# Scratch reads over 128 partitions in column quarters, and a rotation laid out one operation at a time

## What is computed

```
h += 0.5 * swiglu(rms_norm(h), w_in, w_out)      # d_ff 2816
h += mixer(rms_norm(h))                          # layer 0: S5, layer 1: stick-breaking attention
h += 0.5 * swiglu(rms_norm(h), w_in, w_out)
swiglu(h) = (silu(gate) * up) @ w_out            # gate, up = split(h @ w_in)
```

## Time and profile before

| | us |
|---|---|
| median of 3 runs | 1008.85 (1007.89 to 1010.25) |
| the profiled execution | 1011.95 |
| its span | 1010.2 |

### The profile page before, as it was taken

The page is one execution under the profiler, slowest core; times in us unless marked ns, Lnnn a source line. Parts: engine busy times, 40 slices in busy tenths (PEclk is TensorE's granted clock), DMA queues, the critical chain, the costliest instruction groups (busy, mean ns, idle before and its releaser), DMA issues.

```text
span 1010.2 us, 18856 instructions
## 1 busy us (share of the span) xinstructions
PE 986.0 (98%) x7242; PEld 900.6 (89%) x7242; DVE 737.0 (73%) x922; ACT 585.8 (58%) x807; POOL 105.7 (10%) x139
## 2 busy tenths in 40 slices
PE   8998899999999999999999999999999999999997
PEld 8998898988899988888898888888899898888886
DVE  5786786789977777777677777776566687666666
ACT  7543446765355655555456555554599765555555
POOL 4910158100001100000010000001000010000000
PEclk9999999999999999999999999999999999999999
DMA  7879655452246566665646566556643246666563
GB/s 253 216 224 199 185 170 164 145 180 94 63 149 207 163 197 186 192 195 181 198 148 210 188 188 188 188 185 187 191 145 121 88 147 209 189 190 188 194 187 113
DMA packets 50520, 176.89 MB, mean 175 GB/s; under 512 B 7056, under 2 KB 7056, under 8 KB 49936
## 3 DMA queue, kind: packets, MB, share of 16 engines
q1 hardware_dynamic: 50016, 175.32, 57.5%
q10 hardware_dynamic: 432, 0.55, 0.1%
HBM read 174.67 MB, written 1.18 MB: 174 GB/s over the span
## 4 chain that ended last, share of the span: by engine, by line
PE 73%; DVE 10%; DMA 6%; ACT 4%; POOL 4%; issue 3%; SPq 1%; DVEq 0%; POOLq 0%; ACTq 0%
PE mx L1449 11%; PE gu L1449 11%; PE mx L1452 6%; PE gu L1452 5%; DMA raw<-wstream_dram 5%; PE acc L1491 4%; PE gu L1434 4%; PE gu L1435 4%; PE gu L1436 4%; DVE w_lo L909 3%; PE acc L1495 2%; PE gu L1491 2%; ACT w_hi L410 2%; PE mx L1491 2%; PE acc L1478 2%
## 5 line engine op out<-in xcount | busy, mean ns | idle before, releaser
L909 DVE TENSOR_TENSOR w_lo<-raw,w_hi 128x1024 fp32r<-128x1024 f32 x258 | 319.4, 1246 | 107.8 <-ACT w_hi L410 107.1
L410 ACT ACTIVATE w_hi<-raw 128x1024 fp32r<-128x1024 f32 x259 | 271.0, 1052 | 93.5 <-DMA raw<-wstream_dram 34.9
L1434 PE MATMUL gu<-g,w_hi 128*128 128x256 f32 x560 | 161.0, 288 | 4.2 <-DVE w_lo L909 2.4
L1435 PE MATMUL gu<-g,w_hi 128*128 128x256 f32 x560 | 158.4, 283 | 0.0
L1436 PE MATMUL gu<-g,w_lo 128*128 128x256 f32 x560 | 158.3, 283 | 0.0
L1449 PE MATMUL mx<-g,w_hi 128*128 128x512 f32 x480 | 119.9, 392 | 0.0
L1449 PE MATMUL gu<-g,w_hi 128*128 128x512 f32 x464 | 116.1, 392 | 0.0
L1434 PEld LDWEIGHTS gu<-g,w_hi 128*128 128x128 f32 x560 | 107.2, 191 | 5.7 <-issue 3.5
L1435 PEld LDWEIGHTS gu<-g,w_hi 128*128 128x128 f32 x560 | 107.3, 192 | 0.1
L1436 PEld LDWEIGHTS gu<-g,w_lo 128*128 128x128 f32 x560 | 107.2, 192 | 0.0
L1449 PEld LDWEIGHTS mx<-g,w_hi 128*128 128x128 f32 x480 | 87.0, 189 | 16.0
(11 more groups left out here) (325 smaller groups left out, 1912.1 us busy)
## 6 DMA issues: line engine op xcount, KB each, us to landing
raw<-wstream_dram SPq DMA_DIRECT2D x318, 512.0 KB, 3.8
s_memory<-b_turned_dram SPq DMA_DIRECT2D x8, 256.0 KB, 6.6
s_memory<-powers_dram SPq DMA_DIRECT2D x16, 128.0 KB, 8.0
x<-x_in_dram SPq DMA_DIRECT2D x4, 256.0 KB, 6.1
raw<-wstream_dram SPq DMA_DIRECT2D x3, 256.0 KB, 5.8
out_dram<-x_tok SPq DMA_DIRECT2D x3, 256.0 KB, 2.0
gain_row<-last_gain_dram SPq DMA_DIRECT2D x1, 512.0 KB, 4.2
raw<-wstream_dram ACTq DMA_DIRECT2D x1, 256.0 KB, 5.0
```

The lines of the kernel that those rows point to most:

```text
L410: act.activation(weights(unit)[0], raw[:, s_raw, :], ACT.Copy).then_inc(hi_ready, 1)
L909: dve.tensor_tensor(lo, raw[:, n % RAW, :], hi.bitcast(F32), ALU.subtract).then_inc(lo_ready, 1)
L1434: pe.matmul(dst, a, hi, start=start, stop=False, skip_group_check=check)
L1435: pe.matmul(dst, a, lo, start=False, stop=False, skip_group_check=check)
```

## The change

Four things change. The layout of the scratch array: step first, then the half of the pair, so that a store writes two runs (one for each of two steps) where it wrote one. The reads of powers: one copy per unit, over all 128 partitions, of one quarter of the columns (512 floats, 2 KB a row), with the DRAM side as 8 rows each repeated 16 times; the real part comes with units 25 to 28, the imaginary with 29 to 32, each with a counter of its own. The reads of inputs: as many as before, each over 128 partitions and one quarter of the columns, with the DRAM side as 32 rows repeated four times. In the first stage's order, `pad_now` comes one turn earlier (`NOW_TURN` 13), and the six operations of the last doubling stand in turns 18, 19 and 20, one before `scale_gu` and one after it in each, where they stood three and three behind `hidden_low` of turns 18 and 19.

```diff
--- before.py
+++ after.py
@@ -59,7 +59,8 @@
 
 STEP_ARRAYS, S5_ARRAYS = 4, 5
 POWERS_TURNED, POWERS_STORED, POWERS_READ, INPUTS_READ = 5, 24, range(25, 33), range(9, 25, 2)
-OUT_PAD_TURNS, NOW_TURN = (6, 7, 9, 10), 14
+READ_COLS = 512
+OUT_PAD_TURNS, NOW_TURN = (6, 7, 9, 10), 13
 IN_PADS = {17: ((0,), (1,)), 18: ((2,), (3, 4)), 19: ((), (5,)), 20: ((6,), (7,))}
 GROUP, STATE = 16, 64
 PAIRS = 32
@@ -70,7 +71,7 @@
 QP = PAIRS // QUARTERS
 PAIR_ORDER = (0, 4, 1, 5, 2, 6, 3, 7)
 BLOCKS = PAIRS // 4
-FIRST_PRODUCT, KERNEL_TURN, FIRST_ROTATED, DECAY_TURN = 3, 15, 16, 19
+FIRST_PRODUCT, KERNEL_TURN, FIRST_ROTATED, LAST_ROTATED, DECAY_TURN = 3, 15, 16, 18, 19
 SMALL_ROTATIONS = 4
 WARM_UP = 12
 
@@ -229,7 +230,8 @@
         par_ready, par_act, par_dve = sem("par_ready"), sem("par_act"), sem("par_dve")
         powers_ready, dense_ready, padded = sem("powers_ready"), sem("dense_ready"), sem("padded")
         powers_turned, powers_copied = sem("powers_turned"), sem("powers_copied")
-        powers_stored, powers_loaded, inputs_loaded = sem("powers_stored"), sem("powers_loaded"), sem("inputs_loaded")
+        powers_stored, inputs_loaded = sem("powers_stored"), sem("inputs_loaded")
+        powers_loaded = [sem("powers_re_loaded"), sem("powers_im_loaded")]
         c_negated, c_zero_ready, in_dense_ready = sem("c_negated"), sem("c_zero_ready"), sem("in_dense_ready")
         now_cleared, now_dense, in_now_ready = sem("now_cleared"), sem("now_dense"), sem("in_now_ready")
         out_cleared, rot_half = sem("out_cleared"), sem("rot_half")
@@ -315,7 +317,7 @@
 
             return isinstance(i, int) and i == TURNS - 1 and m == BODY - 1
 
-        powers_dram = nc.dram_tensor("powers_dram", (2, STEPS, 2, PAIRS, STATE), F32, kind="Internal").ap()
+        powers_dram = nc.dram_tensor("powers_dram", (STEPS, 2, 2, PAIRS, STATE), F32, kind="Internal").ap()
 
         block = ctx.enter_context(nc.Block())
 
@@ -357,21 +359,22 @@
                 sp.wait_ge(powers_copied, 1)
                 for k in range(2):
                     for g2 in range(2):
-                        sp.dma_start(powers_dram[g2, 2 * k:2 * k + 2].rearrange("j r a p -> (j r a) p"),
+                        sp.dma_start(powers_dram[2 * k:2 * k + 2, g2],
                                      powers_rows[:, P * k + STATE * g2:P * k + STATE * (g2 + 1)]).then_inc(
                             powers_stored, 16)
 
-            def read_powers(r, j):
-                if r == 0 and j == 0:
+            def read_powers(r, part):
+                if r == 0 and part == 0:
                     sp.wait_ge(powers_stored, 16 * 4)
-                for g2 in range(2):
-                    first = CH * j + GROUP * g2
-                    sp.dma_start(powers_t[r][first:first + GROUP, :],
-                                 powers_dram[g2, j, r:r + 1].rearrange("r a p -> r (a p)").broadcast_to(
-                                     [GROUP, PAIRS * STATE])).then_inc(powers_loaded, 16)
-
-            def read_inputs(r, j):
-                sp.dma_start(in_t[r][CH * j:CH * (j + 1), :], b_turned[r]).then_inc(inputs_loaded, 16)
+                cols = slice(READ_COLS * part, READ_COLS * (part + 1))
+                rows = powers_dram[:, :, r].rearrange("j g a p -> (j g) (a p)")[:, cols]
+                sp.dma_start(powers_t[r][:, cols],
+                             rows.unsqueeze(1).broadcast_to([2 * STEPS, GROUP, READ_COLS])).then_inc(powers_loaded[r], 16)
+
+            def read_inputs(r, part):
+                cols = slice(READ_COLS * part, READ_COLS * (part + 1))
+                sp.dma_start(in_t[r][:, cols], b_turned[r:r + 1, :, cols].broadcast_to(
+                    [STEPS, CH, READ_COLS])).then_inc(inputs_loaded, 16)
 
             turns, spread = UNITS // RAW, POWERS_READ[-1] // RAW + 1
             for unit in range(2 * RAW, RAW * spread):
@@ -1095,11 +1098,11 @@
                 real = dense[0].rearrange("p a j h -> p (a j h)")
                 if k == 0:
                     dve.wait_ge(inputs_loaded, 16 * 2 * STEPS)
-                    dve.wait_ge(powers_loaded, 16 * 2 * STEPS)
+                    dve.wait_ge(powers_loaded[0], 16 * STEPS)
                     dve.wait_ge(padded, 4)
                     dve.tensor_tensor(real, powers_t[0], in_t[0], ALU.mult)
                 elif k == 1:
-                    dve.wait_ge(powers_loaded, 16 * 4 * STEPS)
+                    dve.wait_ge(powers_loaded[1], 16 * STEPS)
                     dve.tensor_tensor(spare, powers_t[1], in_t[1], ALU.mult)
                 elif k == 2:
                     step(dve.tensor_tensor(powers_t[0], powers_t[0], in_t[1], ALU.mult))
@@ -1111,19 +1114,28 @@
                     dve.wait_ge(in_dense_ready, 1)
                     dve.tensor_tensor(powers_t[0], real, spare, ALU.subtract).then_inc(in_dense_ready, 1)
 
-            def s5_rotation(k, r):
+            def s5_rotation(k, r, part):
 
                 n = 2 ** k
                 t = [rotation_tmp(k)[:, i, :, 0:n] for i in range(2)]
-                re, im = rot[:, 0, :, 0:n], rot[:, 1, :, 0:n]
+                parts = rot[:, 0, :, 0:n], rot[:, 1, :, 0:n]
                 l_re, l_im = (par[:, i, :].unsqueeze(2).broadcast_to([P, PAIRS, n]) for i in ROTATIONS[k])
-                if r == 0:
-                    dve.tensor_tensor(t[0], re, l_re, ALU.mult)
-                    step(dve.tensor_tensor(t[1], im, l_im, ALU.mult))
+                if part == 0:
+                    dve.tensor_tensor(t[0], parts[r], l_re, ALU.mult)
+                elif part == 1:
+                    step(dve.tensor_tensor(t[1], parts[1 - r], l_im, ALU.mult))
                 else:
-                    dve.tensor_tensor(t[0], im, l_re, ALU.mult)
-                    step(dve.tensor_tensor(t[1], re, l_im, ALU.mult))
-                step(dve.tensor_tensor(rot[:, r, :, n:2 * n], t[0], t[1], (ALU.subtract, ALU.add)[r]))
+                    step(dve.tensor_tensor(rot[:, r, :, n:2 * n], t[0], t[1], (ALU.subtract, ALU.add)[r]))
+
+            def last_rotation(f, part):
+
+                if 0 <= f - LAST_ROTATED < 3:
+                    i = 2 * (f - LAST_ROTATED) + part
+                    if i == 0:
+                        dve.wait_ge(kernels_done, 2)
+                    s5_rotation(SMALL_ROTATIONS + 1, i // 3, i % 3)
+                    if i == 5:
+                        dve.sem_inc(rot_ready, 1)
 
             def read_kernels(half):
                 dve.wait_ge(zeroed, 1)
@@ -1148,22 +1160,21 @@
                     out_product(f - FIRST_PRODUCT)
                 elif 6 <= f - FIRST_PRODUCT < 12:
                     in_product(f - FIRST_PRODUCT - 6)
+                last_rotation(f, 0)
                 scale_gu(f % 2, g0 + 2)
+                last_rotation(f, 1)
                 if KERNEL_TURN < f <= KERNEL_TURN + 2:
                     read_kernels(f - KERNEL_TURN - 1)
                 hidden_high(f % 2, f + 1)
                 split_after(g0 + 1)
                 hidden_low(f % 2, f + 1, f % 2)
-                if 0 <= f - FIRST_ROTATED < 4:
+                if 0 <= f - FIRST_ROTATED < 2:
                     if f == FIRST_ROTATED:
                         dve.wait_ge(rot_started, 1)
-                    if f == FIRST_ROTATED + 2:
-                        dve.wait_ge(kernels_done, 2)
-                    s5_rotation(SMALL_ROTATIONS + (f - FIRST_ROTATED) // 2, (f - FIRST_ROTATED) % 2)
+                    for part in range(3):
+                        s5_rotation(SMALL_ROTATIONS, f - FIRST_ROTATED, part)
                     if f == FIRST_ROTATED + 1:
                         dve.sem_inc(rot_half, 1)
-                    if f == FIRST_ROTATED + 3:
-                        dve.sem_inc(rot_ready, 1)
 
             def add_squares(n):
```

## The result

| | before | after |
|---|---|---|
| median of 13 runs each, us | 1008.77 (1006.2 to 1011.1) | 1011.81 (1010.3 to 1014.2) |
| the profiled execution / its span | 1011.95 / 1010.2 | 1012.66 / 1010.9 |

The ratio is 1.0034 [1.0023, 1.0045]: the change makes the kernel 3.0 us slower by the medians, and 2.3 to 4.5 us by the interval. The forecast was 1003.1, in a range from 996 to 1009, with 0.74 on faster. The profiled execution of before happened to lie 3.2 us above its median and the one after 0.9 above, so the two traces differ by only 0.7 us. They are good for the question where, and the medians for the question how much.

What follows compares the result with a forecast made beforehand. TensorE, busy 98%, was taken as the bound, with waits for h_lo behind late weight loads and slow-clock stretches after them. Terms -4.26 (powers' reads) and -1.4 (rotation), others 0, took 1008.85 to 1003.1 us, range 996 to 1009.

Steps and rivals of the forecast that it cites:

- part 1: Powers' reads on 128 partitions at 275 GB/s, 2.9 us per unit: TensorE's gap at 110.59 and its slow stretch go, -4.26.
- part 3: Input reads as 128 x 2 KB: at most 0.6 us to win, 0 taken; loss bounded by rival B (7 us).
- rival B: Chance 0.14: few engines carry the copies; inputs lose 7.0 us, stores 3.8; +5.1, 1014.0, if an engine moves under 22.8 GB/s.
- Part 2: Stores in two runs on two engines: SP stands about 3 us longer, TensorE's first gap (97.19) stays; value 0.
- The upper end: Bound for the stores: 512 packets take 4.4 us over two engines, 0.54 over sixteen; 3.8 us more.
- The sign that the prediction named for its own error: Weight unit 25 lands so late that TensorE's down unit of turn 7 waits; no size given.
- One gap of over 2 us near 97, none near 110: Sign of being right: TensorE waits over 2 us for h_lo only near 97, with the clock at full after it.
- Part 4: Two counters for the powers: the products of turns 9 and 10 each wait for four reads; cost 0.
- Part 5: NOW_TURN 13: 2.15 us gap at 159.19 goes, VectorE waits 7.0 for GpSimd, not 4.86; value 0, bounds 0 to -2.15.
- Part 6: Last rotation over turns 18 to 20: TensorE gaps 0.78, 0.68, 0.65 go, a 0.7 comes: -1.4 us, bounds 0 to -2.1.
- the new gap of 0.7: At turn 18 h_lo comes near 200.7, where TensorE ends its units at 199.9: a new wait of 0.7 us.
- The sum: -4.26 for the second gap and -1.4 for the rotation make -5.7 us: 1008.85 - 5.7 = 1003.1.

Runs made afterwards that it cites:

- experiment 2: Kernel before with only the new input reads (128 partitions, 2 KB rows, leading repeat of four): 1011.19 us, 1.0038 [1.0021, 1.0055].
- experiment 7: Kernel after with eight stores of 64 rows and input reads from an array holding the rows four times; powers' reads unchanged: 1005.98 us, 0.9972.
- experiment 8: experiment 7 with the powers' reads taking 128 separate rows of the input array (powers' values wrong, for timing alone): 1002.69 us, 0.993.
- experiment 6: Kernel before with 2 KB input reads from an array holding the rows twice, repeated twice (outermost count two): 1029.28 us, 1.0195.
- experiment 3: Kernel before with only the new scratch layout, stores, powers' reads and their counters: 1009.66 us, 1.0012 [0.9998, 1.0027].
- experiment 5: Kernel before with 2 KB input reads over 128 partitions from an array holding the rows four times (outermost count 128): 1006.36 us, 0.9967.
- experiment 9: Kernel before with only the last rotation laid out over turns 18 to 20, NOW_TURN still 14: 1008.51 us, 0.9992 [0.9978, 1.0006].
- experiment 1: Kernel after with all copies and the scratch layout as before; only NOW_TURN 13 and the new rotation left: 1007.92 us, 0.9988 [0.9973, 1.0003].
- experiment 4: Kernel after with eight stores of 64 rows each in place of four stores of two runs: 1009.8 us, 1.0011 [0.9998, 1.0024].
- experiment 10: experiment 5 with NOW_TURN 13 and the stores two units earlier (behind unit 22), old rotation and powers' reads: 1007.0 us, 0.9979.
- experiment 11: experiment 10 with after's scratch layout and powers' reads, and the powers stored by eight copies of 64 rows: 1006.64 us, 0.9976.

## Why the prediction was wrong

**The failed step: part 1 and part 3 priced the reads by partitions and bytes alone.** Part 1 took 275 GB/s at full share for the powers, which supposes all sixteen engines, and part 3 took 0 for the inputs. The shape gave four engines to the inputs and eight to the powers. The inputs' term was 3.8 us (experiment 2) and not 0. In the trace after it begins with the gap of 1.22 at 50.62, and at the down unit of turn 6 TensorE is 2.3 us behind (78.30 for 76.04), 0.4 of it from before 32 us. From experiment 7 to 8, where the powers' reads go from eight engines to sixteen and to another source array, the time falls by 3.3 us. This is rival B; its price for the inputs (7.0) was nearly twice the measured one, its total (+5.1) above the measured +3.0. Its condition is what I weighed wrongly: I held that a lone engine has the others out of its way, and could reach 22.8 GB/s. The loss in experiment 2 and the 20 us of experiment 6 say that it could not; the rate of a single engine was not read. The Trainium skill's rule spoke of all three shapes, and the prediction believed it for the stores alone. The range left B out, though it had 0.14.

**Part 2, the stores: right in kind, too small.** The upper end was 3.8 us more for the landing. What grew was the issue, 5.96 us (8.13 - 2.17), while the wait stayed at 1.9, where 4 to 5 was forecast. I priced the data, and what stood was the third issue (6.15 us); why it stands is not shown. In the trace after that takes units 25 to 27 further back. The sign that the prediction named for its own error, unit 25 so late that the down unit of turn 7 waits, is there in half: that unit waits (1.76 at 88.86), but for unit 24, which was issued ahead of the stores.

**The gaps of parts 1 and 2.** "One gap of over 2 us near 97, none near 110" came true in the pattern (2.75 at 102.76, none at the down unit at 112.95, the clock full from 110 to 114), and was bought with 1.76 and 0.56 ahead of it. The clock falls behind the 1.76 too, so there are two slow stretches in this part as before, only earlier. And VectorE gave part of it back as the prediction allowed: the gap of 0.72 at 130.25 is 1.35 at 132.50. Where -4.26 was forecast for reads and stores together, experiment 3 has +1.2.

**Part 4** cost nothing, as forecast: from 80 to 150 us VectorE waited only for ScalarE, 17.0 us in 20 waits, never for a copy of powers or inputs.

**Part 5** was right about the wait, and too low in its value. The gap at 159 is gone, and most of the gain is given back at GpSimd's tables: VectorE waits 5.84 us there (4.86 in the earlier trace rows, 7.0 forecast). But "nothing of part 5 moves" GpSimd's chain does not hold. From the down unit of turn 12 to the end of that wait it is 41.2 us before and 40.0 after, and over the runs 40.4 to 41.8 with `NOW_TURN` 14 and 40.0 to 40.2 with 13. Why was not looked into. The traces tell parts 5 and 6 apart better than the medians do. From the down unit of turn 12 (139.54 before) to the one that waits for g (221.45 before) they have:

| NOW_TURN | rotation | us, and the runs |
|---|---|---|
| 14 | old | 81.91 (before), 81.87, 81.34, 81.11, 81.93 (experiments 2, 3, 5, 6) |
| 14 | new | 82.43 (experiment 9, with a stretch at the lower clock in it) |
| 13 | new | 80.66 (after), 80.75, 80.64, 80.85, 80.64 (experiments 1, 4, 7, 8) |
| 13 | old | 80.71, 80.66 (experiments 10, 11) |

So `NOW_TURN` 13 is worth 0.4 to 1.3 us here, where 0 stood, and beside it the rotation is worth nothing. VectorE after:

```profile
181.78 0.69 DVE L1124 TENSOR_TENSOR s_memory<-s_memory,par 128x512 f32<-128x512 f32 x1 [5.84 <-POOLq L2197]
...
196.09 1.22 DVE L1124 TENSOR_TENSOR s_memory<-s_memory,par 128x1024 f32<-128x1024 f32 x1
197.32 0.69 DVE L922 TENSOR_TENSOR tmp<-gu,rstd 128x512 f32<-128x512 f32 x1
197.93 1.22 DVE L1126 TENSOR_TENSOR s_memory<-s_memory,par 128x1024 f32<-128x1024 f32 x1
...
200.66 0.42 DVE L936 TENSOR_TENSOR h_lo<-tmp,h_hi 128x256 fp32r<-128x256 f32 x1
203.12 2.36 DVE L912 TENSOR_TENSOR w_lo<-raw,w_hi 128x1024 fp32r<-128x1024 f32 x2 [2.04 <-ACT w_hi L413]
```

**Part 6, -1.4, was too good.** The medians bound it: -1.2 with part 5 (experiment 1), -0.8 alone (experiment 9), neither told from nothing; the last two rows of the table make it about 0. The rows above show the layout as forecast, one operation ahead of the scaling and one behind it. That h_lo of turn 18 stands at 200.66, where 200.7 was forecast, is luck: its turn began 1.0 us late (195.19), and behind that start it comes after 5.5 us and not 6.5, so the new gap of 0.7 is not there either. What the step missed is the next row: VectorE then stands 2.04 us for ScalarE. Why it does is on ScalarE in order of time:

```profile
199.64 0.42 ACT L427 ACTIVATE h_hi<-tmp 128x256 fp32r<-128x256 f32 x1 [0.23 <-DVE tmp L929]
199.96 1.14 ACT L647 ACTIVATE low_part<-s_memory,group_mask 128x1024 f32<-128x1024 f32 x1
201.01 1.13 ACT L647 ACTIVATE s_memory<-s_memory,group_mask 128x1024 f32<-128x1024 f32 x1
202.04 1.99 ACT L413 ACTIVATE w_hi<-raw 128x1024 fp32r<-128x1024 f32 x2
```

Its two pad copies (2.2 us) follow the rounding of the hidden block, which now comes later because the rotation stands ahead of it, and the next units' roundings wait behind them. The gaps 0.78 and 0.68 went (0.17 is left of the two), and the last, 0.65, became 1.88. The 0.72 became 1.05, which is not the rotation's doing: experiments 10 and 11, with the old rotation and `NOW_TURN` 13, have 1.05 and 1.04 there. It makes 2.83 in all before, 3.10 after. The prediction followed VectorE's queue and left out ScalarE's, in which the roundings stand behind the pads.

**The sum** failed by 8.7 us (1011.8 for 1003.1). By the experiments' ratios: 3.8 for the inputs where 0 stood, 1.2 for powers and stores where -4.3 stood, -1.2 for the order where -1.4 stood; this makes 9.5 of difference, with an error of some 2 us on such a sum.

## What to carry to other kernels

Before a copy is turned to reach more partitions, look at its outermost count on both sides: a repeat of rows put ahead of the rows deals the copy over only as many DMA engines as it has repeats. When weights stream beside it, they come late, and the mean DMA share can fall while TensorE waits (0.51 in experiment 6), so a low share is no sign of room. Price an issue as well as a landing: a copy on two engines can hold the issuing queue for microseconds (6.15 here), and all behind it. Where a change has several parts, find two points in the traces that stand on either side of one part only; the distance between them told 0 from 1 us where the medians could not.

## What the hardware showed beside this

- An issue of a narrow copy is itself longer: 0.55 to 0.66 us for an input copy on four engines, mostly 0.43 for the same bytes and rows on sixteen (experiment 5), and 0.58 to 0.64 for a powers copy on eight.
- The granted clock is at 0.50 through the rows 90.00:93.40, 103.60:107.00 and 223.10:226.50. Where TensorE is full, such a stretch costs about 1.4 us, by the prediction's reckoning from the earlier trace rows; the last one cost 0.3 at most by the S5 mixer. Such stretches stood behind gaps of 1.76 to 3.09 us, but gaps of 2.36 (experiment 1), 2.53 (experiment 4) and 2.52 (experiment 7) had none behind them. The same gap of 1.88 or 1.89 before the tail has one in after and in experiments 1 and 8, and none in 4, 7 and 9. So one execution differs from the next by a term that the gap alone does not give.
- Over 77.5 to 110 us, with the powers going onto 16 neighbouring partitions, the kernel before had 203 GB/s at a share of 0.96; with them going onto 128, on sixteen engines, experiment 8 had 242 at 0.75. In time of the engines that is 323 for 211.
